# A hybrid decoder trunk on one core: the output stored in quarters, the last expert unit's down products by output half over four back banks, and a unit's last activations in two halves

## The reference, cut to what matters

```python
def swiglu(x, w_gate, w_up, w_down):
    return (jax.nn.silu(x @ w_gate) * (x @ w_up)) @ w_down

def moe_swiglu(xn, w_router, we_gate, we_up, we_down):
    logits = (xn @ w_router).astype(jnp.float32)
    top_v, top_i = lax.top_k(logits, TOP_K)          # TOP_K = 2, N_EXPERTS = 8, D_FF = 3584
    top_w = jax.nn.softmax(top_v, axis=-1)
    gates = jnp.sum(jax.nn.one_hot(top_i, N_EXPERTS, dtype=jnp.float32) * top_w[..., None], axis=-2)
    y = jnp.zeros_like(xn)
    for e in range(N_EXPERTS):
        y = y + gates[..., e:e + 1].astype(xn.dtype) * swiglu(xn, we_gate[e], we_up[e], we_down[e])
    return y
# in reference(): h = h + moe_swiglu(rms_norm(h, ln_ffn1), ...), and h is the output
```

## Time and profile before

| | |
|---|---|
| runs | 1530.54, 1535.26 and 1529.33 us, median 1530.54 |
| profiled execution | 1527.4 us, of which its span is 1525.6 |
| TensorE busy | 1464.8 us (96%) |
| weight loads | 1221.0 us (80%) |
| VectorE, ScalarE, GpSimd busy | 1211.0 (79%), 1050.3 (69%), 40.8 us (3%) |
| memory | 433.54 MB read, 7.86 MB written, 289 GB/s over the span |
| granted TensorE clock | 0.987 of full speed on average |

### The profile page before, as it was taken

The page is one execution under the profiler, slowest core; times in us unless marked ns, Lnnn a source line. Parts: engine busy times, 40 slices in busy tenths (PEclk is TensorE's granted clock), DMA queues, the critical chain, the costliest instruction groups (busy, mean ns, idle before and its releaser), DMA issues.

```text
span 1525.6 us, 22113 instructions
## 1 busy us (share of the span) xinstructions
PE 1464.8 (96%) x7056; PEld 1221.0 (80%) x7056; DVE 1211.0 (79%) x1584; ACT 1050.3 (69%) x1395; POOL 40.8 (3%) x83
## 2 busy tenths in 40 slices
PE   6998999999988899999999999999999999999995
PEld 5987888888886788878878878888888888887883
DVE  6957655555565689989989989989988988998993
ACT  5664644444584377887787778878778778788772
POOL 1000000000000000000000010000000000000000
PEclk9999999999998999999999999999999999999997
DMA  8554365555242469999999999999999999999990
GB/s 270 165 180 138 139 220 182 186 195 162 66 166 77 172 240 384 378 355 387 377 351 382 390 350 386 384 360 373 380 384 346 393 381 352 389 377 350 396 393 34
DMA packets 191802, 442.02 MB, mean 290 GB/s; under 512 B 8750, under 2 KB 20364, under 8 KB 191756
## 3 DMA queue, kind: packets, MB, share of 16 engines
q1 hardware_dynamic: 188636, 429.90, 77.8%
q0 software_dynamic: 3120, 11.54, 2.7%
HBM read 433.54 MB, written 7.86 MB: 289 GB/s over the span
## 4 chain that ended last, share of the span: by engine, by line
PE 90%; DVE 5%; ACT 3%; issue 1%; DMA 0%; ACTq 0%; SPq 0%; DVEq 0%
PE bank L465 86%; PE bank L1025 2%; DVE w_lo L1613 1%; ACT w_hi L1130 1%; DVE xT_lo L1655 1%; DVE aT_lo L2274 0%; PE bank L751 0%; ACT aT_hi L1519 0%; PE bank L477 0%; DMA late<-in_mem_dram 0%; PE bank L656 0%; ACT scr L1467 0%; DVE stat L1634 0%; DVE stat L1632 0%; DVE stat L1633 0%
## 5 line engine op out<-in xcount | busy, mean ns | idle before, releaser
L1613 DVE TENSOR_TENSOR w_lo<-raw,w_hi 128x1024 fp32r<-128x1024 f32 (+1 forms) x832 | 958.6, 1197 | 175.5 <-ACT w_hi L1130 160.2
L1130 ACT ACTIVATE w_hi<-raw 128x1024 fp32r<-128x1024 f32 (+1 forms) x832 | 839.9, 1043 | 216.0 <-PE bank L465 210.8
L465 PE MATMUL bank<-w_hi,xT_hi 128*128 128x512 f32 (+4 forms) x1358 | 529.7, 390 | 12.3 <-DVE w_lo L1613 4.4
L465 PE MATMUL bank<-w_hi,xT_lo 128*128 128x512 f32 (+4 forms) x1358 | 521.8, 384 | 0.0
L465 PE MATMUL bank<-w_lo,xT_hi 128*128 128x512 f32 (+4 forms) x1358 | 521.2, 384 | 0.0
L465 PEld LDWEIGHTS bank<-w_hi,xT_hi 128*128 128x128 f32 x1358 | 255.9, 188 | 63.8 <-issue 8.6
L465 PEld LDWEIGHTS bank<-w_hi,xT_lo 128*128 128x128 f32 x1358 | 255.7, 188 | 49.6
L465 PEld LDWEIGHTS bank<-w_lo,xT_hi 128*128 128x128 f32 x1358 | 256.0, 189 | 46.0
L465 PE MATMUL bank<-w_hi,aT_hi 128*128 128x512 f32 x544 | 214.1, 394 | 5.8 <-DVE aT_lo L2274 5.8
L465 PE MATMUL bank<-w_lo,aT_hi 128*128 128x512 f32 x544 | 214.1, 394 | 0.0
L465 PE MATMUL bank<-w_hi,aT_lo 128*128 128x512 f32 x544 | 211.6, 389 | 0.0
(11 more groups left out here) (354 smaller groups left out, 763.0 us busy)
## 6 DMA issues: line engine op xcount, KB each, us to landing
raw<-in_we_gate_dram SPq DMA_DIRECT2D x112, 1024.0 KB, 7.7
raw<-in_we_up_dram SPq DMA_DIRECT2D x112, 1024.0 KB, 7.9
raw<-in_we_down_dram SPq DMA_DIRECT2D x112, 1024.0 KB, 6.9
raw<-in_w_gate_dram SPq DMA_DIRECT2D x14, 1024.0 KB, 5.1
raw<-in_w_up_dram SPq DMA_DIRECT2D x14, 1024.0 KB, 5.1
raw<-in_w_down_dram SPq DMA_DIRECT2D x14, 1024.0 KB, 4.8
raw<-in_w_in_dram SPq DMA_DIRECT2D x16, 768.0 KB, 4.9
raw<-in_w_out_dram SPq DMA_DIRECT2D x8, 1024.0 KB, 5.2
```

The costliest lines, as they stand in the source:

```text
L465: return pe.matmul(o, a, b, start=start, stop=stop, skip_group_check=True, **kw)
L1130: act.activation(split_piece(w_hi, c, shape, half), raw_piece(c, shape, half), ACT.Copy).then_inc(hi_ready, 1)
L1613: dve.tensor_tensor(split_piece(w_lo, c, shape, half), raw_piece(c, shape, half), F(split_piece(w_hi, c, shape, half)), ALU.subtract).then ...
```

## The change

It has four parts.

- The store is made in four parts, (half, t) in the order of `QUARTERS`, each when VectorE has counted its addition in `h_added`. SyncE waits for `h_final` only if there are overflow units.
- Unit 7's last down product (`e_down_end` with `by_columns`) does all of output half 0 (bank 4) and counts `y_half`, then all of half 1 (bank 5). ScalarE scales half 0 on `y_half`. `back` takes the halves in order, each on its own wait, over four banks (6, 7, 0, 1) without waiting for an addition; the wait for additions stands ahead of an overflow unit.
- In every unit the last turn goes by halves: two transposes into bank 2, two into bank 6; ScalarE and VectorE work on 128x256 each, and the first down products wait for the first half only. `e_high` and `e_low` count 6 steps for a unit in place of 7 and are left for the other steps.
- `e_in` at a unit's start waits for the first four of `xT_lo`, and for the other four ahead of its third piece.

```diff
+        QUARTERS = ((0, 0), (0, 1), (1, 0), (1, 1))
+        back_bank = lambda half, t: B[(6, 0)[half] + t]
...
-            sp.wait_ge(sem("h_final"), 1)
-            sp.dma_start(out.rearrange("o (b p) d -> p (o b) d", p=P), h[:, :, :]).then_inc(sem("stored"), 16)
-            sp.wait_ge(sem("stored"), 16)
+            n_over = sp.value_load(unit_i[0:1, 3:4], min_val=0, max_val=NU_MAX)
+            with sp.If(n_over > 0):
+                sp.wait_ge(sem("h_final"), 1)
+            out_v = out.rearrange("o (b p) d -> p (o b) d", p=P)
+            for n, (half, t) in enumerate(QUARTERS):
+                sp.wait_ge(sem("h_added"), n + 1)
+                cols = slice(half * 512, (half + 1) * 512)
+                sp.dma_start(out_v[:, t, cols], h[:, t, cols]).then_inc(sem("stored"), 16)
+            sp.wait_ge(sem("stored"), 16 * len(QUARTERS))
...
-            def e_in(c, which, more):
+            def e_in(c, which, more, gathered=None):
                 for j in range(4):
+                    if gathered is not None and j % 2 == 0:
+                        pe.wait_ge(sem("gather_ready"), gathered + j // 2 + 1)
...
+            def e_turn_halves(n):
+
+                pe.wait_ge(sem("eact_done"), n + 1)
+                for q in range(FB):
+                    last = pe.transpose(B[(2, 6)[q // 2]][:, (q % 2) * P:(q % 2 + 1) * P], act_f[:, q * P:(q + 1) * P],
+                                        ident[:, :])
+                    if q % 2:
+                        last.then_inc(sem("eaT_half_psum"), 1)
+
+            def e_down_end(c, more, u, by_columns):
+
+                def product(j, half):
+                    w = [split_piece(x, c + j // 2, DOWN, j % 2) for x in wS]
+                    for a, b in TERMS:
+                        last = mm(B[4 + half][:, :], aT[a][:, j, 0:P], w[b][:, 0, half * 512:(half + 1) * 512],
+                                  start=False, stop=(j == 3 and (a, b) == TERMS[-1]))
+                    return last
+
+                def ready(j):
+                    if j % 2 == 0:
+                        pe.wait_ge(sem("eaT_half"), 2 * u + j // 2 + 1)
+                    pe.wait_ge(lo_ready, 2 * c + j + 1 + 2 * more)
+
+                if by_columns:
+                    for half in range(2):
+                        for j in range(4):
+                            if half == 0:
+                                ready(j)
+                            last = product(j, half)
+                            if half == 1:
+                                last.then_inc(piece_used, 1)
+                        if half == 0:
+                            last.then_inc(sem("y_half"), 1)
+                    return
...
             def back(v):
 
-                pe.wait_ge(sem("ys_ready"), 2 * v + 2)
                 pe.wait_ge(sem("onehotT_ready"), v + 1)
-                for t in range(TB):
-                    for half in range(2):
-                        if t:
-                            pe.wait_ge(sem("h_added"), 4 * v + half + 1)
...
+                for half, t in QUARTERS:
+                    if t == 0:
+                        pe.wait_ge(sem("ys_ready"), 2 * v + half + 1)
...
-                    e_down(c + 4, m, n0 + i, start, False)
+                    e_down(c + 4, m, (NF - 1) * u + i, start, False)
...
-                e_turn(n0 + NF - 1)
+                e_turn_halves(n0 + NF - 1)
                 if not last:
                     gathered_turned(u + 1)
-                e_down(C_MOE + 40, more, n0 + NF - 1, False, True)
+                e_down_end(C_MOE + 40, more, u, last)
...
-                e_high(n0 + NF - 1)
+                for b in range(2):
+                    act.wait_ge(sem("eaT_half_psum"), 2 * u + b + 1)
+                    act.activation(aT_hi[:, 2 * b:2 * b + 2, 0:P], B[(2, 6)[b]][:, 0:2 * P].rearrange("p (q s) -> p q s", q=2),
+                                   ACT.Copy).then_inc(sem("eaT_half_hi"), 1)
...
-                e_low(n0 + NF - 1)
+                for b in range(2):
+                    dve.wait_ge(sem("eaT_half_hi"), 2 * u + b + 1)
+                    dve.tensor_tensor(aT_lo[:, 2 * b:2 * b + 2, 0:P], B[(2, 6)[b]][:, 0:2 * P].rearrange("p (q s) -> p q s", q=2),
+                                      F(aT_hi[:, 2 * b:2 * b + 2, 0:P]), ALU.subtract).then_inc(sem("eaT_half"), 1)
```

More of the change, by code:

```diff
@@ L1086, in unit @@
                     return
-                pe.wait_ge(sem("gather_ready"), 2 * u + 4)
-                e_in(C_MOE + FFN_CHUNKS, 0, more)
+                e_in(C_MOE + FFN_CHUNKS, 0, more, gathered=2 * u + 2)
                 pe.wait_ge(sem("y_scaled"), 2 * u + 2)
@@ L1094, in _ @@
             keep_busy(22, 6)
[L1095 to L1096 removed]
+            e_in(C_MOE, 0, 0, gathered=0)
             with pe.Fori(0, NE - 1) as u:
```

35 lines of the change are left out of this document (18 added, 17 removed).

## The result

The changed kernel takes 1520.96 us, median of five runs (1518.62 to 1522.2), against 1530.54 us, median of five runs of the kernel before on the same chip (1528.43 to 1535.26). The ratio is 0.993, with a 95% interval from 0.9911 to 0.9948. That is 9.6 us less, where 9.0 were forecast, and faster by more than 0.5%. The profiled execution took 1521.53 us, of which its span is 1519.8.

The account below looks back on a forecast made before the run. TensorE was taken as the bound, in the expert stage and in its three branches at the end. 2.75 + 0.7 + 5.0 + 0.55 = 9.0 us off the median of 1530.54 gave 1521.5 us, range 1517 to 1528.

Parts of the forecast that it names:

- What ends the span: At the program's end, TensorE's three branches over overflow-unit code fill the last 15.0 us; the store is not last.
- Store in quarters: Final store in four parts: counted at nothing, since SyncE is done 2.8 us before TensorE already.
- The end of the last unit: From the last of 24 down products to reading unit_i: 1.7 us instead of 4.45, a gain of 2.75 us.
- The last turn: Last unit's activations in halves: shorter transposes, ScalarE copy and VectorE subtraction gain 0.7 us.
- The borders: The same halves at the seven other unit borders: 7 x 0.72 = 5.0 us, bounded per border by 0.45 to 0.85.
- The first unit: First unit's gathered rows in halves: TensorE starts after four of eight xT_lo, gaining 0.55 us, bounds 0 and 1.1.
- Added instructions: Extra register instructions in TensorE's 48 steps and ahead of ScalarE's silu: taken as nothing; uncovered, 1.5 us.
- Borders give half: Rival at the unit borders: 5.0 becomes about 1 to 2.5 us, time 1524 to 1526; chance 0.12.
- Code fetched again: Rival: TensorE's longer outer loop is no longer held, seven returns cost 22 us, time 1543; 0.04 including other losses as large.
- Something else ends it: Rival: TensorE's end branches come out shorter, so VectorE or the store ends last; 1519.5 to 1521 us; chance 0.06.
- Longer branches: Rival at the end: TensorE's branches lengthen beside the quarters by 1.4 us, up to 2.9; time 1523 to 1524.5; chance 0.16.
- The sum: Whole kernel: 9.0 us gained, span 1525.6 to 1516.6, median 1530.54 to 1521.5 us.

Follow-up runs that it names:

- e_store_only: The kernel before with only the store in quarters on the additions' count, in its own order of additions; 1531.73 us, ratio 1.0005 to the kernel before.
- both nested kernels: The kernel before and the changed kernel, each with the three overflow tests nested on TensorE and VectorE, so one jump skips all: 1524.81 and 1514.22 us.
- e_halves_only: The changed kernel with store, `back`, additions and last down product as before, leaving only the halves at last turns and `e_in`; 1523.95 us, ratio 0.9965 to before.
- e_one_store: The changed kernel with the single store behind `h_final` in place of quarters; 1520.70 us, ratio 0.994 to the kernel before.
- e_early: The changed kernel with nested overflow tests moved ahead of the last unit's scaling, `back` and additions on TensorE and VectorE; 1511.58 us, ratio 0.9868 to before.

## Why the prediction was right, point by point

- **What ends the span.** Right, and shown twice: the store can be moved by 6 us without effect (e_store_only), and taking branches away moves the time (both nested kernels). A fetch of code stands in the trace within every one of the branches. The chain of waits ends at the last addition in either profile and doesn't show this; the order of the drains does.
- **Store in quarters, at nothing.** Right in size, 0.26 us between medians with quarters and without, in favour of neither. The estimate from the Trainium skill ("DMA: Bandwidth & Descriptors", anatomy of one DMA), 10.4 us for four stores one after the other, doesn't hold here: from the first quarter's issue at 1504.74 to SyncE's drain at 1510.7 it takes 6.0 us. That section of the Trainium skill gives its figures for DMAs that GpSimd issues. They make an estimated 2.6 us for one quarter. The first three, issued by SyncE, took 2.62, 2.68 and 2.75 us, the fourth 3.99. What fails is that they follow each other, which the prediction had left open.
- **The end of the last unit, 2.75.** Measured 2.90, from the start of the last down product. The prediction puts the columns first and doesn't divide the gain; the runs show that the four banks carry the greater part (2.18 alone against 1.71).
- **The last turn, 0.7.** Measured 0.70, here and in e_halves_only.
- **The borders, 7 x 0.72 = 5.0.** Measured 7 x 0.70 = 4.9. The row-by-row sum held because the nearest rows were of the same size and source: 0.379 became 0.382, and 0.414 became 0.420. The first border lost nothing against the last, so the halves didn't meet the slower weights, though ScalarE's waits for them doubled (3.0 us in place of 1.4 for one matrix, 2.8 in place of 1.3 for another).
- **The first unit, 0.55.** Measured 0.67: the first product follows the fillers 0.1 us sooner than I had allowed.
- **Added instructions, nothing.** No part shows them.
- **The rivals.** *Borders give half* fell to 0.70 each. *Code fetched again* fell: the loop's return takes 67 to 209 ns, and no block of code comes while the loop runs. *Something else ends it* fell. *Longer branches* is true in kind and small in size: the first branch went from 3.58 to 4.18, and the three together are 0.3 longer, less than the 1.4 of that rival; against e_one_store, the same kernel but for the store, it is 0.9 in single profiles. Its mechanism, a store beside the jump, is the one that the pairs above bear out. One reading against it was wrong: the third branch was said to run beside no store, but the old store landed only at 1522.3, 1.7 us into it.
- **The sum.** 9.0 forecast and 9.6 measured between medians, 9.2 by the parts. The parts bear the sum out term by term. That the medians agree to 0.6 us is partly luck, as the median of the kernel before itself came out between 1530.2 and 1532.2 in the other sets of runs. What the prediction had wrong is its span of 1516.6, which was 1519.8: the profiled pair gave 5.8 us, largely by a clock that was lower in a stretch where TensorE's program had not changed.

## What to carry to other kernels

Look at the order in which the engines drain before spending work on the last store: an engine's sequencer may be last with branches that no busy time and no chain of waits shows. On TensorE, tests over code that is not run should jump once, and be taken while the engine still has products queued for as long as the jump lasts. Where a copy and a subtraction stand between two stretches of TensorE, halves of them are worth their shortened durations, as long as the next wait behind them has that much idle time; in this kernel the rows of nearest size gave it to a few hundredths of a microsecond.

## What the runs showed of the hardware

- A taken jump of TensorE over one body of a unit or over three cost 3.5 to 5.5 us and brought in one or two blocks of 16 KB on a queue called instruction; taken behind queued products, with a second read of the count, it cost 0.8. The returns of a loop of some 525 instructions took 67 to 233 ns and brought in none.
- The other engines pay less for the same three tests: behind a branch over one body VectorE's sequencer stood for 0.1 to 2.0 us and ScalarE's for 0.1 to 1.1. Behind one jump over three bodies VectorE's stood for 2.8 to 4.1.
- Four stores of 256 KB, issued about 0.6 us apart, overlapped (2.6 to 2.8 us for each of the first three, 4.0 for the last, 6.0 in all); one store of 1 MB took from 4.0 to 5.9, the more where TensorE was taking its branches at the same time.
- The time of a run follows its mean granted clock: for e_halves_only 1520.92 us at 0.987 and 1530.9 at 0.978, for e_early 1508.76 at 0.992 and 1519.36 at 0.983. A hundredth of the clock goes with some 11 us here, more than the whole change, so single runs could not have settled it.
